# Two layers of attention on one core: the projections of six forgetting-attention head pairs by Strassen's scheme

## The reference

```python
def fox_mixer(h, w_in, b_f, w_out):
    proj = h @ w_in                       # 1024 x 1024 by 1024 x (4*1024 + 16)
    q, k, v, z = ...                      # 16 heads of 64 each
    log_f = jax.nn.log_sigmoid((f_logit + b_f).astype(jnp.float32))
    c = jnp.cumsum(log_f, axis=1)
    # for each block of 128 queries:
    s = jnp.einsum('bqhd,bkhd->bhqk', qi, k) * FOX_HEAD_DIM ** -0.5
    s = s + ci[..., None] - ck[:, :, None, :]          # causal mask, then softmax
    o = jnp.einsum('bhqk,bkhd->bqhd', softmax(s), v)
    return (o * jax.nn.silu(z)) @ w_out
```

## Time and profile before

| | |
|---|---|
| median of 3 runs | 2823.71 us (2823.36 to 2826.67) |
| profiled execution | 2817.91 us, its span 2816.1 us |
| TensorE busy | 2697.2 us, 96% of the span |
| VectorE, GpSimd, ScalarE busy | 1439.6, 1351.2, 979.9 us |
| mean granted TensorE clock | 0.98 |
| fox pairs 3 to 7, from one gate Tanh to the next | 75.6 to 75.8 us each |
| fox pair 8 (nothing to project) | starts at 1318.7 us |

### The profile page before, as it was taken

One profiled execution on the slowest core, in us unless ns is written; L12 is line 12 of the kernel. 1 busy time (PEld: TensorE's weight loads), 2 busy tenths in 40 slices (PEclk: granted clock), 3 DMA queues, 4 the chain that ended last, 5 costly groups with the idle time before them and its releaser, 6 DMA issues.

```text
span 2816.1 us, 42376 instructions
## 1 busy us (share of the span) xinstructions
PE 2697.2 (96%) x16872; PEld 2077.9 (74%) x16872; DVE 1439.6 (51%) x3044; ACT 979.9 (35%) x1857; POOL 1351.2 (48%) x797
## 2 busy tenths in 40 slices
PE   7999988989899999999999999999999999999998
PEld 5766675668677777776788777777878777776886
DVE  6979998556633333334434665343433434345323
ACT  5322412562333343434321324333333333333112
POOL 2543383034222222223543238777777777776541
PEclk8999998999999999999999999999999999999999
DMA  4101021031111111112112111111111111114211
GB/s 114 43 23 30 23 71 60 8 120 39 54 49 49 53 53 46 53 53 83 53 53 78 57 38 46 53 42 42 46 53 54 46 49 36 53 46 151 75 45 68
DMA packets 222464, 155.66 MB, mean 55 GB/s; under 512 B 26374, under 2 KB 209068, under 8 KB 222140
## 3 DMA queue, kind: packets, MB, share of 16 engines
q1 hardware_dynamic: 211196, 122.55, 15.1%
q10 hardware_dynamic: 11072, 30.39, 3.0%
HBM read 133.45 MB, written 19.47 MB: 54 GB/s over the span
## 4 chain that ended last, share of the span: by engine, by line
PE 49%; DVE 1%; issue 1%; ACT 1%; POOL 0%; ACTq 0%; DVEq 0%; POOLq 0%
PE proj L1534 8%; PE proj L1536 8%; PE proj L1535 8%; PE proj L1054 5%; PE proj L1056 5%; PE proj L1055 5%; PE out L1604 3%; PE score L1565 2%; PE score L1584 1%; PE out L1055 1%; PE out L1056 1%; PE out L1054 1%; PE out L1573 0%; PE proj L1549 0%; DVE arena L2602 0%
## 5 line engine op out<-in xcount | busy, mean ns | idle before, releaser
L880 POOL TENSOR_TENSOR w_hi<-w_raw,ones 128x1024 fp32r<-128x1024 f32 x105 | 254.3, 2422 | 967.4 <-PE proj L1056 955.5
L1054 PE MATMUL proj<-act_hi,w_hi 128*128 128x512 f32 x1440 | 588.1, 408 | 10.4 <-ACT arena L2025 5.0
L1056 PE MATMUL proj<-act_hi,w_lo 128*128 128x512 f32 x1440 | 569.2, 395 | 0.0
L1055 PE MATMUL proj<-act_lo,w_hi 128*128 128x512 f32 x1440 | 569.1, 395 | 0.0
L1054 PEld LDWEIGHTS proj<-act_hi,w_hi 128*128 128x128 f32 x1440 | 275.8, 192 | 78.8 <-issue 15.5
L1056 PEld LDWEIGHTS proj<-act_hi,w_lo 128*128 128x128 f32 x1440 | 275.1, 191 | 60.5
L1055 PEld LDWEIGHTS proj<-act_lo,w_hi 128*128 128x128 f32 x1440 | 276.2, 192 | 52.8 <-issue 0.2
L882 POOL TENSOR_TENSOR w_lo<-w_raw,w_hi 128x1024 fp32r<-128x1024 f32 x105 | 268.0, 2552 | 8.2
L2123 ACT ACTIVATE arena<-proj 128x512 f32<-128x512 f32 x140 | 133.7, 955 | 395.2 <-PE proj L1536 395.1
L2765 DVE SCALAR_TENSOR_TENSOR arena<-proj,arena 128x512 f32<-128x512 f32 x140 | 136.2, 996 | 259.4 <-PE proj L1536 259.4
L981 POOL TENSOR_TENSOR w_lo<-w_raw,w_hi 128x512 fp32r<-128x512 f32 x140 | 181.9, 1299 | 179.5 <-ACT w_hi L2108 176.7
(11 more groups left out here) (310 smaller groups left out, 5099.7 us busy)
## 6 DMA issues: line engine op xcount, KB each, us to landing
w_raw<-dil_w_in_dram SPq DMA_DIRECT2D x140, 256.0 KB, 3.5
w_raw<-fox_w_in_dram SPq DMA_DIRECT2D x32, 512.0 KB, 4.1
w_raw<-w_in_dram SPq DMA_DIRECT2D x23, 512.0 KB, 3.6
y_scratch<-arena ACTq DMA_DIRECT2D x21, 512.0 KB, 3.6
act_lo<-y_scratch SPq DMA_DIRECT2D x21, 512.0 KB, 6.1
arena<-decay_scratch ACTq DMA_DIRECT2D x16, 512.0 KB, 5.6
w_raw<-ple_w_gate_dram SPq DMA_DIRECT2D x16, 512.0 KB, 3.8
arena<-x_dram SPq DMA_DIRECT2D x12, 512.0 KB, 4.9
```

Source lines behind the costliest of these rows:

```text
L880: pool.tensor_tensor(hi, raw, one.unsqueeze(1).broadcast_to([P, KB, P]), ALU.mult).then_inc(w_hi_done, 1)
L1054: pe.matmul(bank, hi, a_hi, start=first, stop=False)
L1055: pe.matmul(bank, hi, a_lo, start=False, stop=False)
L1056: return pe.matmul(bank, lo, a_hi, start=False, stop=last)
```

## The change

The projections of fox pairs 3 to 8 (made during the attention of pairs 2 to 7) use Strassen's scheme. Each pair has two "tile pairs", (query, key) and (gate, value), of 7 units each: 14 units of 12 matmuls. One unit stands in the opening, one in step 0, two in each of steps 1 to 5 (one where the first part was, one where the second was), one each in steps 6 and 7 (where the second part was; the first part's place is empty). The value transposes move to the start of the next pair, right behind its first scores. Pairs 1 and 2 are projected as before.

What comes with it:
- VectorE makes three sums of activation quarters during pair 1 (44 operations of 128x512 over its eight steps) and the fourth at the start of pair 2 (12 operations after the gate, 4 more after the rows of tile 2; ScalarE rounds the results in between, 4 operations right behind the exponential of tile 1). The fourth unit of pair 2 (in step 1) waits for the last of them.
- `hT` is written to `x_scratch` (4 MB) before pair 1 and loaded again when the last unit is done.
- GpSimd works on quarters of weights for pairs 3 to 8, as in the dil layer.
- `unit_out` of ScalarE stands behind the gate Tanh and ahead of the copy of the first transposes; the unit at the head of a step is put out ahead of that step's exponential.
- The output goes into the gate's buffer; `vT` shares the buffer of the Tanh.

```diff
-SUM_ROLES = ((("q", 0), ("q", 1)), ...)
+SUM_ROLES = dict(dil=((("q", 0), ("q", 1)), ...),
+                 fox=((("q", 0), ("k", 0)), (("g", 0), ("vT", 0))))
...
+def fox_units(p, t):
+
+    first = UNITS * len(SUM_ROLES["fox"]) * (p - 1)
+    if t == 0 or t > 5:
+        return [], [first + (t + 6 if t else 1)]
+    return [first + 2 * t], [first + 2 * t + 1]
...
@@ TensorE, one pair @@
                     scores(0, 0)
+                    if kind == "fox" and p > 1:
+                        for half in range(2):
+                            turned_values("fox", p - 2, half)
...
-                    if follow and kind == "fox":
+                    if follow and summed:
+                        unit("fox", UNITS * len(SUM_ROLES["fox"]) * (p - 1))
+                    elif follow and kind == "fox":
                         project(next_pair(kind, p), [pair_units(kind, p, 0)[1]])
...
-                        if follow:
+                        if follow and summed:
+                            for n in fox_units(p, i)[0]:
+                                unit("fox", n)
+                        elif follow:
                             project(next_pair(kind, p), head + ([] if first_part is None else [first_part]))
...
+                        if i == 0 and kind == "fox" and p > 1:
+                            later(pe, SUM["fox"], "xe", 2 * (p - 1))
@@ ScalarE, one pair @@
+                    if kind == "fox" and p > 1:
+                        for half in range(2):
+                            values_turned("fox", p - 2, half)
                     exp(0)
...
                     act.activation(R["e"], Q["g"], ACT.Tanh, scale=0.5).then_inc(S["gate"], 1)
+                    if follow and summed:
+                        unit_out("fox", UNITS * len(SUM_ROLES["fox"]) * (p - 1))
                     for i in range(NT):
                         turned(i, 0)
-                        if follow:
+                        if follow and summed:
+                            for n in fox_units(p, i)[0]:
+                                unit_out("fox", n)
...
                         if i + 1 < NT:
                             exp(i + 1)
+                        if kind == "fox" and p == 1 and i == 0:
+                            for k in range(KB // 2):
+                                fox_fourth_hi(k)
@@ VectorE, one pair @@
+                        if kind == "fox" and p == 0:
+                            (fox_sums_12, fox_sums_3)[t % 2](t // 2)
+                            if t == NT - 1:
+                                fox_lo(KB // 2 - 1, 2)
+                        if kind == "fox" and p == 1 and t < 2:
+                            if t == 0:
+                                for half in range(2):
+                                    dve.wait_ge(pass_done[half], C_FOX + 10)
+                            for k in range(KB // 2):
+                                (fox_fourth, fox_fourth_lo)[t](k)
+                        if summed:
+                            for n in sum(fox_units(p, t), []):
+                                unit_out("fox", n)
...
+            def fox_fourth(k):
+                x, y = act_words[:, 0, k, 512:1024], act_words[:, 1, k, 512:1024]
+                hi, lo = sum_operand("fox", 1)
+                dve.tensor_tensor(x, hi[:, k].bitcast(F32), hi21, ALU.subtract).then_inc(ST["tv"], 1)
+                dve.tensor_tensor(y, lo[:, k].bitcast(F32), lo21, ALU.subtract).then_inc(ST["tv"], 1)
+                later(dve, ST, "tv", done + 2)
+                dve.tensor_tensor(y, x, y, ALU.add).then_inc(ST["tv"], 1)
@@ TensorE, unit @@
+                if m_ == 0 and j in (2, 3):
+                    later(pe, ST, "tl", (12, 16)[j - 2])
@@ SP @@
                 if m == 1:
                     finished_rows("fox", C_FOX)
+                    sp.dma_start(hT[:, :, :], xd).then_inc(xback, 16)
                     late_row("fox")
@@ ScalarE, before pair 1 @@
-                    projected(0, 0, halves[4:])
+                    projected(0, 0, halves[4:5])
+                    later(act, NF, "back", 2 * KB)
+                    act.dma_start(xd, hT[:, :, :]).then_inc(xsent, 16)
+                    projected(0, 0, halves[5:])
```

More of the change, by code:

```diff
@@ L538, in build @@
         fields["dil"]["e"] = vT[0]
-        w_sum = [DL.take(512).rearrange("p (k c) -> p k c", c=P) for _ in range(2)]
+        w_sum = dict(dil=[DL.take(512).rearrange("p (k c) -> p k c", c=P) for _ in range(2)])
         def dil_set(p):
@@ L772, in finished_rows @@
                 m = MIXER[kind]
-                if kind == "dil":
-                    later(sp, ST, "unit", UNITS_ALL)
+                if kind in SUM:
+                    later(sp, SUM[kind], "unit", UNITS_ALL[kind])
                 else:
@@ new lines, in turned_values @@
+            def turned_values(kind, x, half):
+                ST, done = SUM[kind], turned_after(kind, x)
+                natural = kind == "fox" or x % 3 == 0
+                source = fields["fox"]["vT"] if kind == "fox" else vT[0]
+                if half == 0:
+                    later(pe, ST, "ed", 5 * done - 1)
+                else:
+                    later(pe, ST, "ea", 4 * done)
+                for n in range(4):
+                    at = half * 512 + n * P if natural else n * DIL_SPAN + half * P
+                    mm = pe.transpose(proj[(done + half) % 2][:, n * P:(n + 1) * P], source[:, at:at + P], ident[:, :])
+                mm.then_inc(ST["x"], 1)
@@ L1319, in out_rows @@
                     pe.wait_ge(w_split, n + 1)
[L1320 to L1322 removed]
+                    units_left("dil")
                 for j in js:
@@ L2011, in projected @@
                         role, g = roles[b]
+                        if kind == "fox" and p == 1 and role == "vT":
+                            act.wait_ge(S["gate"], 2 * (before + 1))
                         if role == "vT":
@@ L2682, in one @@
                         finish(NT - 1, p - 1, set_of(kind, p - 1))
+                    summed = kind == "fox" and p > 0 and follow
+                    if summed:
+                        unit_out("fox", UNITS * len(SUM_ROLES["fox"]) * (p - 1))
                     for t in range(NT):
```

591 lines of the change are left out of this document (350 added, 241 removed).

## The result

The changed kernel takes 2830.25 us (median of 14 runs, 2826.84 to 2836.21), the kernel before 2823.48 us beside it (14 runs): ratio 1.0026, 95% interval 1.0018 to 1.0034. It is slower; the prediction said 2815 (2802 to 2828) and faster. The profiled execution has a span of 2831.1 us, 15.0 more than that of before; the execution profiled before took 2817.91 us, less than all 14 runs of its kernel, so the two profiles lie further apart than the medians do. TensorE works less, as meant (18.7 us less busy time), VectorE and GpSimd more.

A forecast was written before the change was run, and what follows sets the result against it. TensorE was taken as the bound, busy 2697.2 of 2816.1 us. Terms -34.4 + 5.4 + 2.5 + 3.0 + 0.5 + 13.7 = -9.3 took the median 2823.71 to 2814.4, stated as 2815; 8-in-10 range 2802 to 2828.

The forecast's parts named there:

- The matmuls that go: Steps 6 and 7 of six pairs: 24 fewer matmuls a pair save 5.74 us each, 34.4 us in all.
- Steps 6 and 7: Halved cover: waits of 0.5 at tile 7's second scores and 0.4 at the second transposes, 5.4 us for six pairs.
- The opening: Start of a pair: 0.5 us wait at unit 0's bank (2.5 in all), 0.5 before the first values (3.0 in all).
- Pair 2's long wait: Step 1: unit 3 waits 12 us for the fourth sum, GpSimd mostly idle; slower clock adds 1.7, together 13.7 us.
- The three sums in pair 1: VectorE's sums, 3.1 to 3.7 us a step, fit in gaps; 0.5 us put for steps 6 and 7.
- the wait for `w_lo`: Sign on TensorE: if waits on `w_lo` appear, GpSimd is the bound and the prediction is wrong; no size given.
- Pair 7, -3.9: Stretch from pair 7's Tanh to the next: predicted 3.9 us shorter.
- Pair 8, nothing: Stretch from pair 8's Tanh to the first output matmul: predicted difference 0.
- The load of `hT`: Reload of 4 MB begun in pair 7's last step, done about 30 us into pair 8; costed at nothing, 1 to 8 if late.
- The rival "VectorE against GpSimd everywhere": All pairs: contention costs VectorE 13 us a pair, a quarter on the path; +10 us, 2834; chance 0.15.

The follow-up runs named there:

- Experiments 2: The changed kernel with GpSimd, in its first weight tile of pair 2, waiting until VectorE has made the fourth sum; ratio 1.0034 to the kernel before.
- 6: The changed kernel with the fourth sum's low parts straight behind its 12 operations and GpSimd held off twice in pair 2; ratio 1.0003 to the kernel before.
- 5: The changed kernel with VectorE's four low parts of the fourth sum straight behind its 12 operations; ratio 1.0015 to the kernel before.
- Experiment 3: The changed kernel with GpSimd's splits of the output weight's first two blocks earlier and one tile apart; ratio 1.0012 to the kernel before.
- 8: The changed kernel with the moves of 6 and Experiment 3, `hT` reloaded behind later weight blocks, and pair 2's units shifted by a tile; ratio 1.0026.
- 9: The changed kernel with the moves of 6 and Experiment 3, and `hT` reloaded between the last attention row and the weight blocks; 2816.18 us, ratio 0.9979.
- experiment 14: The changed kernel itself, timed and profiled a second time with nothing altered; 2830.62 us, ratio 1.0038 to the kernel before.

## Why the prediction was wrong, by its own steps

- *The matmuls that go, 5.74 us a pair.* Right: by distance of starts, waits left out, the projection matmuls of pair 5 take 46.2 us before and 40.5 after. Yet pairs 3 to 6 gained 3.5 each, not 3.9, although TensorE's idle time rose by only 1.4 (from 75.60 - 74.80 to 72.20 - 70.01) where 1.9 were predicted. A term is missing from the sum: where a projection group no longer follows, `spread` and the transposes stand further apart, 0.8 us a pair that is no wait (`spread` 0.45 before and 0.85 after, the value transposes 0.85 and 1.09, those of the rows 7.95 and 8.12). That the pair came out within 0.4 us is partly luck, a missing 0.8 against waits priced 0.5 too high.
- *Steps 6 and 7, 0.9 a pair.* Only one wait of 0.38 came, at the second scores of tile 7 (0.5 predicted); the 0.4 at the second transposes didn't.
- *The opening, 0.5 and 0.5.* 0.34 at unit 0's bank, and 1.32 before the first values where the earlier trace rows has 0.72, so 0.6. Right.
- *Pair 2's long wait, 12 + 1.7.* The place, the releaser and the clock behind it were right; it took 16.88 + about 1.7. The first failed step is the sentence that GpSimd "is mostly idle there, having used up what TensorE has freed". It worked without a pause from 869.17 to 888.9, so the 12 operations that I priced at 7.8 took 13.7. Experiments 2 and 6 show that part; 5 shows that the place of the last four costs 3.8 besides. That GpSimd was so late, because its wait for VectorE's last sum stands ahead of quarters that were ready 6.5 us sooner, is read from the kernel and the trace; no run takes that wait away.
- *"The three sums in pair 1: 3.1 to 3.7 us of VectorE a step ... I put 0.5."* The second failed step, wrong by 3.8; the 0.5 were expected in steps 6 and 7, and nothing came there. Beside a weight split two of a step's sums took 2.88 and 2.89 instead of 0.69, over 4 us more, and TensorE waited 0.94 and 1.82 where it hadn't waited at all. Halving the splits gives 2.3 us back (83.6 to 81.3) and leaves 0.58 of these two waits; 0.96 is the wait for `w_lo`, which the prediction had named as a sign of being wrong, and some 0.5 is no wait.
- *Pair 7, -3.9.* The third failed step, a term put at nothing without a reason: the output weight's splits had run inside pair 7 and now wait for the last unit, so both fall into the opening of pair 8, beside its decays. It cost 4.1. Experiment 3 takes the wait away, and then pair 7 gains 6.5, more than the 3.9 forecast, since TensorE then stands idle for 2.2 us of the stretch where it stood 3.4 in the kernel before.
- *Pair 8, nothing.* +2.8: GpSimd's 128x1024 low parts meet VectorE's small operations. TensorE's waits rose by 1.3 in all; the rest goes with the 3.4 us of half clock behind the longest. That the two engines meet is shown; the wait was 3.04 in the changed kernel and 4.56 to 4.91 in experiments 2, 3, 5, 6, 8 and 9, as what ends earlier or later moved the meeting, and I can't forecast it to the microsecond.
- *The load of `hT`, nothing.* In the changed kernel no wait shows it, in the kernel before it cost 0.34% with the save. I had looked at who reads `hT`, not at whose small store stands behind it.
- *The rival "VectorE against GpSimd everywhere"*, 2834 at 0.15, was the nearest. Its mechanism was right, its distribution not: pairs 3 to 6 lose nothing, four single places lose all.

By the table, the mis-sized terms are +5.2 (pair 2), +3.8 (pair 1), +4.1 (pair 7), +2.8 (pair 8) and +1.7 (pairs 3 to 6): 17.6, which turns -9.3 into +8.3. The other 6.8 us of the profile lie ahead of pair 1 and in the rest, where nothing was changed but the save and the reload of `hT`, and 4.7 of them did not come again in experiment 14. The medians, over 14 runs each, differ by 6.8.

## What to carry to other kernels

Before costing new work on VectorE, write down what GpSimd does in the same microseconds and how long one of its instructions is: each VectorE operation with two SBUF inputs can cost one whole GpSimd instruction, however small it is. A helper that had to wait for another engine comes back with its backlog just when that engine goes on (here 20 us without a pause). Where both must run, order them by a wait (and look where the held work lands then), or cut GpSimd's instructions in two at that place only; and put a large transfer behind the small one that somebody waits for.

## What was not expected of the hardware

- A 128x128 operation of VectorE took up to 2.4 us and a 128x512 one 2.9 us beside GpSimd operations of 2.4 to 2.7 us, in turn: one of the one, one of the other. A 128x512 GpSimd operation went from 1.27 to 1.75 us in the same way.
- A plain `COPY` of 128x128 with a single SBUF input was held too (0.23 us alone, 1.87 and 0.92 beside GpSimd), while operations on PSUM and one SBUF operand were not. The Trainium skill (SBUF — State Buffer, "Who interferes with whom") lists copies among the operations that can take the shared pair; the trace agrees.
- Behind one and the same stop of 4.4 us the granted clock of 20 us was 0.91 or 0.74 in two executions of the same kernel, 4.7 us of 2830. So a difference of 5 us between two single profiles needs to be looked up by stretch before it is put down to a change.
